# A two-block decoder on one core: the forget gate's slab ahead of the keys, three splits ahead of two slabs, a one-slab index key, and a memory softmax of both halves at once

## What is computed

```python
# first block
(pr, pk, pv, pwd, pad_, z_a, q, ckv, z_b, qi, ki, wi, g_a, g_b) = split(shifted(h @ w_in))
y_a = rwkv7_branch(...)                                    # 8 heads of 64
# inside dsa_branch: ki is 64 columns (index keys), wi is 8 columns (a weight per index head)
s_idx = relu(einsum('bqhd,bsd->bqhs', qi, ki)); score = einsum('bqh,bqhs->bqs', wi, s_idx)
y_b = dsa_branch(q, ckv, qi, ki, wi, ...)                  # top 64 keys, then softmax
merged = sigmoid(g_a) * ((y_a * silu(z_a)) @ w_pa) + sigmoid(g_b) * ((y_b * silu(z_b)) @ w_pb)
x = x + gate * (merged @ w_o)
# second block
x = x + 0.5 * rmsnorm(swiglu(...))
q_a, f_a, i_a, g_a, q_b, k_b, v_b, f_b, gates = split(rmsnorm(x) @ w_in_2)
o_a = rmsnorm(hgrn2_chunkwise(q_a, f_a, i_a)) * silu(g_a)
c = cumsum(log_sigmoid(f_b + bias))                        # f_b: 8 columns, the forget gate
o_b = softmax(q_b k_b^T / sqrt(128) + c_t - c_s) v_b       # causal, 8 heads
x = x + rmsnorm((gate0 * (o_a @ w_branch_a) + gate1 * (o_b @ w_branch_b)) @ w_out)
x = x + rmsnorm(softmax(q k^T / 16) v @ w_mo)              # memory attention, 4 heads of 256
x = x + 0.5 * rmsnorm(swiglu(...))
```

## Time and profile before

| | us |
|---|---|
| median of 3 runs (lowest, highest) | 1280.08 (1278.33, 1281.07) |
| the profiled execution | 1280.07, of which the span is 1278.3 |
| PE busy | 1181.5 (92%) |
| POOL busy | 920.2 (72%) |
| ACT busy | 597.5 (47%) |
| DVE busy | 464.4 (36%) |
| mean granted clock of PE | 0.971 |

### The profile page before, as it was taken

How to read it: one execution, slowest core, us unless ns; L and a number is a source line. 1 busy time by engine, 2 the same in 40 slices (tenths; PEclk the granted TensorE clock), 3 DMA queues, 4 the chain that set the end, 5 groups by cost and what they waited for, 6 DMA issues and landing times.

```text
span 1278.3 us, 21358 instructions
## 1 busy us (share of the span) xinstructions
PE 1181.5 (92%) x8446; PEld 997.1 (78%) x8446; DVE 464.4 (36%) x828; ACT 597.5 (47%) x872; POOL 920.2 (72%) x931
## 2 busy tenths in 40 slices
PE   7999899999799999999999997899998988999997
PEld 7889898677577788787887875777777967888785
DVE  5618536664444111102435664532233033111101
ACT  5354333433645544534544435475436335544533
POOL 3779834442378888786899996468798827888784
PEclk8899989999899999999999998899999989999999
DMA  9897422332245566565564553345566514666562
GB/s 327 236 275 198 132 68 88 112 117 84 95 168 165 181 184 184 170 193 159 139 175 134 149 149 103 96 118 164 195 232 180 150 50 151 195 182 183 167 197 94
DMA packets 183939, 202.63 MB, mean 159 GB/s; under 512 B 7544, under 2 KB 142112, under 8 KB 183072
## 3 DMA queue, kind: packets, MB, share of 16 engines
q1 hardware_dynamic: 178624, 186.31, 49.0%
q10 hardware_dynamic: 5216, 14.97, 3.3%
HBM read 197.03 MB, written 4.21 MB: 157 GB/s over the span
## 4 chain that ended last, share of the span: by engine, by line
PE 65%; POOL 16%; issue 6%; ACT 5%; DVE 5%; DMA 2%; SPq 1%; POOLq 0%; ACTq 0%; DVEq 0%
PE ps L685 18%; PE ps L687 17%; PE ps L686 17%; POOL wlo L2626 16%; PE ps L682 11%; PE ps L690 3%; ACT whi L1292 1%; DMA raw<-in_w_in 1%; ACT L1292 1%; DMA raw<-in_w_mkv 1%; DVE gt L1843 1%; DVE acc L1851 0%; ACT hThi L1292 0%; DVE x L1851 0%; DVE hE L1843 0%
## 5 line engine op out<-in xcount | busy, mean ns | idle before, releaser
L2626 POOL TENSOR_TENSOR wlo<-raw,whi 128x256 fp32r<-128x256 f32 (+1 forms) x922 | 914.8, 1026 | 343.7 <-ACT whi L1292 340.1
L1292 ACT ACTIVATE whi<-raw 128x1024 fp32r<-128x1024 f32 x325 | 342.1, 1057 | 350.8 <-PE ps L687 308.9
L685 PE MATMUL ps<-whi,hThi 128*128 128x512 f32 (+2 forms) x672 | 270.0, 402 | 11.9 <-POOL wlo L2626 6.2
L687 PE MATMUL ps<-whi,hTlo 128*128 128x512 f32 (+2 forms) x672 | 260.8, 388 | 0.0
L686 PE MATMUL ps<-wlo,hThi 128*128 128x512 f32 (+2 forms) x672 | 260.2, 387 | 0.0
L685 PE MATMUL ps<-hThi,whi 128*128 128x256 f32 x576 | 168.8, 293 | 14.9 <-issue 8.0
L686 PE MATMUL ps<-hTlo,whi 128*128 128x256 f32 x576 | 163.7, 284 | 0.0
L687 PE MATMUL ps<-hThi,wlo 128*128 128x256 f32 x576 | 163.5, 284 | 0.0
L685 PEld LDWEIGHTS ps<-whi,hThi 128*128 128x128 f32 x672 | 128.1, 191 | 44.1 <-issue 18.1
L687 PEld LDWEIGHTS ps<-whi,hTlo 128*128 128x128 f32 x672 | 128.1, 191 | 26.8
L686 PEld LDWEIGHTS ps<-wlo,hThi 128*128 128x128 f32 x672 | 128.4, 191 | 22.0
(11 more groups left out here) (381 smaller groups left out, 1555.9 us busy)
## 6 DMA issues: line engine op xcount, KB each, us to landing
raw<-in_w_in SPq DMA_DIRECT2D x121, 512.0 KB, 3.8
raw<-in_ffn_w_in SPq DMA_DIRECT2D x176, 256.0 KB, 3.2
raw<-in_ffn_w_down SPq DMA_DIRECT2D x44, 512.0 KB, 4.3
raw<-in_w_mkv SPq DMA_DIRECT2D x16, 512.0 KB, 6.1
raw<-in_ada_w SPq DMA_DIRECT2D x8, 512.0 KB, 5.9
raw<-in_w_o SPq DMA_DIRECT2D x8, 512.0 KB, 3.7
raw<-in_w_branch_a SPq DMA_DIRECT2D x8, 512.0 KB, 3.6
raw<-in_w_branch_b SPq DMA_DIRECT2D x8, 512.0 KB, 3.7
```

What stands on the lines that cost most here:

```text
L685: e.matmul(o, l[0], r[0], start=start, stop=False)
L687: return e.matmul(o, l[1], r[0], start=False, stop=stop)
L1292: return e.activation(o, i, f, **k)
L2626: p = e.tensor_tensor(wlo[c % NHL][:, o], raw[i % NRAW][:, o], whi[c % NHL][:, o], ALU.subtract)
```

## The change

It does seven things to the plan and to the streams:

- One slab (columns 3840 to 3968) gives both the 64 index keys and the 8 head weights. PE then copies the keys to partitions 64 to 128 by a matmul with an identity and transposes the head weights (`wi_turn`), after the first slab of za0, and `wi_out` on DVE evacuates both. The second slab, its unit and the wi unit are gone.
- The forget gate's slab `fb` comes after qb and ahead of kb.
- Three splits, with the `finish` of the chains that they need, stand ahead of the last slabs of the units that they used to follow: ya two slabs ahead (before g3's third), yb one slab ahead (before pa1's second and last), oa two slabs ahead (before gt3's third).
- `memlog` makes the logits of both halves of rows, then the softmax of both, and then the transposes of both.
- A preload of the square root's table stands ahead of w_out's units, and in `post_out` ACT rounds the next slab ahead of the first post's square root. That holds for w_out and for w_mo.
- Relu steps of dsa on ACT are grouped by two.
- The planner treats DVE and then ACT of a step as one after the other, where it took both from the end of PE's part, and a started or opened chain is ready no earlier than DVE.

```diff
+    def before(self, grp, kh, *what):
+        k = max(i for i, d in enumerate(self.todo) if d[0] == "unit" and d[1].grp == grp and d[1].kh == kh)
+        self.todo[k:k] = what
...
-    "memlog": [(1.8, 1.4, 0), (1.8, 1.4, 0), (0, 2.6, 2.2), (1., 1.4, 0), (0, 2.6, 2.2), (1., 1.4, 0)] + [(1.8, .7, .6)] * 4,
+    "memlog": [(1.8, 2.6, 0), (1.8, 2.6, 2.8), (0, 1.4, 2.8), (1., 2.8, 0), (1., 1.4, 0)] + [(1.8, .7, .6)] * 4,
...
-        i = fm("ki", w, 3776, 128, "ki", None)
-        self.todo[-1][1].w, self.todo[-1][1].last = 2, False
-        i = self.slab([(None, w[:, 3840:3968].rearrange("(k p) n -> p k n", p=P))], (8, 128))
-        self.unit("fm", i, "ki", "ki", None, j=1, w=2, keep=True)
-        self.unit("wi", i, "wi", "wi", None)
-        do("start", "dsa")
+        fm("ki", w, 3840, 128, "ki", None)
...
+            if j == 0:
+                k = max(i for i, d in enumerate(self.todo) if d[0] == "unit" and d[1].grp == "za0" and d[1].j == 0)
+                self.todo.insert(k + 1, ("wi",))
+                self.todo.insert(k + 2, ("start", "dsa"))
...
-        do("finish", "rwkv", "head0", "head1")
-        do("split", "ya")
+        self.before("g3", 2, ("finish", "rwkv", "head0", "head1"), ("split", "ya"))
...
-        do("finish", "dsa")
-        do("split", "yb")
+        self.before("pa1", 1, ("finish", "dsa"), ("split", "yb"))
...
+        fm("fb", w, 7168, 128, "fb", None, gen=3)
         for j in range(4):
             fm(f"kb{j}", w, 5120 + 256 * j, 256, "copy", ("kb", 2 * j), gen=3)
         for n in range(2):
             tm(f"v{n}", w, [(6144 + 512 * n, 512)], "tmcopy", ("vb", n), gen=3)
-        fm("fb", w, 7168, 128, "fb", None, gen=3)
         do("start", "fox")
...
-        do("finish", "hgrn")
-        do("split", "oa")
+        self.before("gt3", 2, ("finish", "hgrn"), ("split", "oa"))
...
+        do("table")
         for n in range(2):
             tm(f"wout{n}", rows["w_out_2"], [(512 * n, 512)], "post", ("mix", n, "gt"), gen=4)
...
                 if n:
-                    now[e] = max(now[e], now["pe"]) + n
-                    ready[c] = max(ready[c], now[e])
+                    now[e] = max(now[e], ready[c]) + n
+                    ready[c] = now[e]
...
-                    at[c], ready[c] = 0, now["pe"] + 0.5
+                    at[c], ready[c] = 0, max(now["pe"] + 0.5, now["v"] + 0.2)
...
+                if d[0] in running and at[d[0]] >= limit[d[0]]:
+                    ready[d[0]] = max(ready[d[0]], now["v"] + 0.2, now["a"] + 0.2)
...
+            def wi_turn():
+                b = bank("main", ("wi",), "ev_v")
+                w.wait_ge(S["ev_v"], ("ki",))
+                mm(b[64:128, 0:256], ident[0:64, 0:64], kiT[0:64, :])
+                for t in range(2):
+                    m = e.transpose(b[:, 256 + 8 * t:264 + 8 * t], kiT[64:72, t * 128:t * 128 + 128], ident[64:72, 64:72])
...
                 if u.arg[1] == 1:
+                    if t == 0:
+                        round_slabs(place[u.slab] + u.ahead + 1)
                     post(u.arg[0], t)
...
+            def wi_out():
+                w.wait_ge(S["mm"], ("acc", "wi"))
+                b = PS[bank_of["wi",]]
+                cp(wi[:, :, :], b[:, 256:272].rearrange("p (t h) -> p t h", t=2))
+                cp(kiT[64:128, :], b[64:128, 0:256]).then_inc(S["ev_v"].tick(("wi",)), 1)
```

60 lines of the change are left out of this document (27 added, 33 removed).

## The result

The changed kernel takes 1266.51 us (median, 1260.97 to 1268.06) where the kernel before takes 1280.16 in the same comparison: a ratio of 0.988 with an interval of 0.985 to 0.991, or 13.6 us less. The forecast was 38 us less, 1242. The way is right and the size is not: a third of the gain came.

The account below looks back on a forecast made before the run. PE was taken as the bound, busy 1181.5 of 1278.3 us, with gaps and half clock to recover. Terms 12 + 2 + 1 + 11 + 4.4 + 4.7 + 3 = 38 off 1280.07 gave 1242, with 1228 to 1257 for 8 in 10.

Parts of the forecast that it names:

- three signs of being wrong: Run of steps idles over 12 us, hgrn stops PE over 5 at the forget gate, or mean clock stays 0.97.
- the run of steps: Last steps of head0, head1 and dsa, ahead of g3's third slab without units among them: 5 to 7 us PE idle.
- The index keys, 12: Wi unit 7.7 and second key slab 2.9 saved, 2.8 of clock returned, less 0.7 new work; 12 us taken.
- The split of ya, +2: Waits for x and yalo with slow work, 9.4 us, go; the run of steps costs 7.4; net +2.
- The forget gate, 8 net: Early fb slab removes PE's wait for lfr and slow work, 10 us, less 2 for fb stopping hgrn.
- Later steps, +5 for the fox stage: Planner's steps about half a unit later shrink fox and hgrn waits; half of 9.5 us, taken as 5.
- The second rival: The waits move: forget gate gives 2 instead of 11, oa split 2 instead of 4.4; 1253 us, 20 in 100.
- The split of oa, 4.4: Two slabs behind the split cover PE's wait for oalo, 2.8 us, plus 1.6 of slow work.
- w_out, 4.7: Table loaded ahead and slab rounded first: PE's wait of 4.0 and 1.7 slow work go, less 1.0 later norm.
- The memory softmax, 3: Both halves' logits first, so exponentials overlap and the last chain starts earlier: 3 us, between 1 and 6.5.
- The first rival: The clock doesn't come back: half-clock shares of about 12 us are not gained; 1254 us, 12 in 100.
- the forecast's seven stretches: Seven short stretches at 1.2 GHz, six beginning at PE gaps the edits aim at, one in 128x8 matmuls.

Follow-up runs that it names:

- keys_alone: The kernel before with the one-slab index keys and nothing else: 1273.83 us, ratio 0.995.
- round_early: The changed kernel with ACT rounding the next slab right behind each projection unit's second half, ahead of the chain steps: 1282.98 us.
- one_source: The changed kernel with w_o's addition taking one operand from PSUM and the post norms' two-column sum made a one-source reduction: 1258.93 us, ratio 0.983.
- late_both: one_source with the forget gate's slab back behind v and no early rounding at the post norms: 1253.99 us, ratio 0.979.
- mixed_plan: one_source without early rounding, forget gate's slab early, and the planner's old model from the first feed-forward's norm on: 1247.57 us, ratio 0.972.
- before_one_source: The kernel before with one_source's two edits, w_o's addition from PSUM and the sum as a reduction: 1273.89 us, ratio 0.996.

## Why the prediction missed

Stretch by stretch, the 24.5 us between forecast and measurement are these, by the first profile: 1.7 ahead of q3, which is chance; 0.8 in block one from there; 5.5 between w_o and qb3; 9.0 from qb3 to ba0, where 15.4 were forecast and 6.4 came; 1.1 from there to wmo1; 4.9 behind w_mo; and 1.5 in the second feed-forward, where the clock fell for 3.4 us behind a wait of 1.88 that the kernel before has too. Two of the forecast's three signs of being wrong came true: hgrn stopped PE by over 5 us at the forget gate (5.16), and the mean clock stayed at 0.971. The third didn't, for the run of steps idled by 4.3 us and not by over 12.

- **The index keys, 12.** The instructions and the clock went as said: no 128x8 matmuls, 1.00 from 150 to 175. The step that failed is that the whole sum stays on the path: alone it left 5.3 us from q3 on, because the chains set the end of the stage (keys_alone). Together with the split of ya more of it stays, so that the two terms can't be told apart in the changed kernel.
- **The split of ya, +2.** The steps were right (waits of 7.6 us gone, waits of 1.88, 0.89 and 1.25 in the run of steps), but both sides of the balance were mis-sized. The run idled for 4.3 us, not 5 to 7, and the clock fell in it for 3.4 us, which costs 1.7. What it removes is more than the 9.4 of the kernel before: with the shorter keys and the late split the waits are 2.55 and 7.13, with 6.1 us of work at half clock around them, half of which is a loss. It is worth 7 to 10. By luck this cancels the keys' miss: at wo1 the changed kernel is 12.5 us ahead, or 14.2 from q3 on, where 15 was forecast for both with yb.
- **The forget gate, 8 net.** With the old steps it measures 7.2, up to gt0 as up to ba0: right, and the stop of hgrn (5.16 us, or 4.16 with the old steps) lay inside its 0 to 8. Against that, the slab's own 3.7 us only moved, from behind v to a stretch where POOL sets the pace.
- **Later steps, +5 for the fox stage.** This is the step that failed most. The sign is wrong: with the slab early they cost 4.7 us there, and beside them the slab's move is worth 1 to 3. The waits for z1f went and waits for POOL came. For two of the three (1.97 and 2.45) it is shown that chain steps on ACT, which came to stand ahead of the rounding, make them (round_early); the third (2.77) goes with the old steps too, by a way that is open. This and the double counting of one wait are some 9 to 11 us of the 24 missed. The second rival put the gate and oa together at 4 us in place of 15.4, and 4.7 (one_source) to 6.4 came: it is that rival's outcome, by another mechanism.
- **The split of oa, 4.4.** 3.6 in its stretch, 2.1 from bb0 on: right in kind, somewhat small.
- **w_out, 4.7.** The wait for POOL fell from 4.02 to 1.77 in the first profile (3.8 us won), and nothing was won in the second, where the add behind it was starved for 4.99. Two steps failed. The wait of 4.02 was put down to ACT's table load and root ahead of the rounding, and a starved add of 2.19 us was in it: without starvation the kernel before takes 40.9 us for the stretch, where late_both takes 40.2 and mixed_plan 41.9, so that the table's preload alone wins nothing that can be seen. And "the cost is about 1 us of later norm" left out what a POOL that goes on does to DVE.
- **The memory softmax, 3.** 3.2 us, which is the forecast's number, but as a sum of two: with the old steps the stretch is 6.0 us shorter than before, and the later steps take some 3 of them back, for which the forecast had no term. Behind it, w_mo had the early rounding too, which the forecast didn't price: gaps of 2.70 for 1.65, and a fall of the clock, 4.9 us together (2.2 in the second profile, where the fall was 3 us long and not 10).
- **Behind w_o**, 5.0 us are lost to one starved instruction, in a stretch that no edit touches. The forecast had no term and no rival for it. After the later steps this is what cost most: DVE's additions were taken to last as long as in the kernel before, and one of 1 us took 14.59.
- **The clock.** The first rival was right in its sum: the shares at half clock, 12 us in the forecast, didn't come back; the mean is 0.971 in both (0.975 in the second profile). At the keys the clock did come back, and at oa's first gap too; the falls moved to other waits, and more of PE's work lies in them (66.1 us for 55.4). The earlier trace rows don't hold all falls of the kernel before: there are three in the first 55 us and one of 3.4 us at 669.4, behind a wait of 2.02 for POOL, which the forecast's seven stretches leave out. With fewer waits the falls grow fewer: mixed_plan's mean is 0.981.

Not undone one by one were the split of yb, the grouped relus, the order of the memory softmax and the table's preload. Their shares are argued from the stretches and not shown.

## What to carry to other kernels

Where POOL runs without a break, list the DVE instructions with two SBUF operands on the path, and turn them to one operand in PSUM or one source; a change that feeds POOL better can lengthen them. Two edits that aim at one wait are one term of a sum, and the gain of work taken off the busiest engine is to be followed to the next place where that engine waits for a chain. A planner's rule that helps in a stage paced by chains can cost in one where the same engine also prepares the next slabs.

## What the runs showed of the hardware

- A DVE instruction with two SBUF operands can miss every change of POOL's instructions: 14.59, 14.62 and 16.57 us for one of 0.69, 4.97 to 4.99 for one of 0.16, each ended with POOL's run. In the same run of POOL others get in after one instruction (1.21 in place of 0.69). What decides between the two isn't settled; no run here varied the moment at which DVE asks. The traces give one hint: of the ten DVE instructions of 128x512 that took over 3 us in the sixteen profiles, nine began 0.48 to 0.64 us into one of POOL's instructions of 0.74, and one began 0.07 us into it. Others that began 0.48 to 0.57 us into one took 0.72 to 0.82, so this alone doesn't decide.
- With an operand in PSUM the same addition took 0.69 us beside 47 us of unbroken POOL work, and all forty of these additions in the ten profiles with that edit took the same, with POOL at work or not.
- The granted clock fell for 10 us with PE busy all the time in the kernel before, in 128x8 matmuls. It did so again in before_one_source (158.3 to 168.5), and none of the fourteen profiles without these matmuls has a fall from 150 to 175. Every other fall past the first 60 us, in all sixteen profiles, stands at or shortly behind a wait of PE of 1 us or more. But not every wait has one, and not in every execution: behind w_mo it fell for 10 us in one profile of the changed kernel and for 3 in the other.
